# Issuing the attention's loads of later heads from ScalarE's queue instead of SyncE's

## The reference

```
h = RMSNorm(x);  proj = h @ w_in            -> a, gate, q, k, v
group A: u = a*sigmoid(gate); depthwise causal conv (31); LayerNorm; silu; @ w_pw
group B: 8 heads of 64; q, k normed per head; beta = sigmoid(q.k/8)
         A[t,s] = beta[t,s] * prod_{s<j<t} (1 - beta[t,j]),  s < t;   o = A @ v
x = x + concat(A, B) @ w_out;   x = x + relu(RMSNorm(x) @ w_ff1)^2 @ w_ff2
```

## Time and profile before

| | us |
|---|---|
| runs | 2756.15, 2759.61, 2755.06 (median 2756.15) |
| the profiled execution, its own time | 2761.99 |
| its span, first to last instruction | 2760.2 |

### The profile page before, as it was taken

How to read it: one execution, slowest core, us unless ns; L and a number is a source line. 1 busy time by engine, 2 the same in 40 slices (tenths; PEclk the granted TensorE clock), 3 DMA queues, 4 the chain that set the end, 5 groups by cost and what they waited for, 6 DMA issues and landing times. The chain is left out here.

```text
span 2760.2 us, 36720 instructions
## 1 busy us (share of the span) xinstructions
PE 2663.6 (96%) x13304; PEld 2223.3 (81%) x13304; DVE 1797.6 (65%) x2824; ACT 1121.9 (41%) x2221; POOL 592.7 (21%) x523
## 2 busy tenths in 40 slices
PE   8988899999999999999999999999999999999999
PEld 6757778788887887788888797778777877889998
DVE  6996777577773576377775358736888851755444
ACT  4434524455552122355554112334666630333342
POOL 2222210022220010032221002103333310533230
PEclk9999999999999999999999999999999999999999
DMA  9795797697669568455554746854455447355452
GB/s 330 254 351 191 233 354 279 252 332 267 254 219 371 225 228 280 177 218 186 178 181 157 305 183 224 269 197 155 145 191 175 162 161 293 123 189 177 168 198 96
DMA packets 294750, 616.14 MB, mean 223 GB/s; under 512 B 23665, under 2 KB 188529, under 8 KB 250029
## 3 DMA queue, kind: packets, MB, share of 16 engines
q1 hardware_dynamic: 294573, 613.80, 62.8%
HBM read 444.79 MB, written 168.94 MB: 222 GB/s over the span
## 5 line engine op out<-in xcount | busy, mean ns | idle before, releaser
L1277 POOL TENSOR_TENSOR beta<-beta,stay 128x512 f32<-128x512 f32 (+3 forms) x328 | 319.1, 974 | 882.2 <-DVE stay L2047 850.9
L2297 PE MATMUL ps<-h2T_hi,w_s 128*128 128x512 f32 (+2 forms) x976 | 369.6, 379 | 7.6 <-DMA w_s<-w_scratch 3.5
L2299 PE MATMUL ps<-h2T_hi,w_s 128*128 128x512 f32 (+2 forms) x976 | 359.2, 368 | 0.0
L2298 PE MATMUL ps<-h2T_lo,w_s 128*128 128x512 f32 (+2 forms) x976 | 358.7, 367 | 0.0
L1581 ACT ACTIVATE stay<-ps 128x512 f32<-128x512 f32 (+3 forms) x328 | 174.7, 533 | 343.7 <-PE ps L2498 213.3
L2570 PE MATMUL ps<-w_s,hid_hi 128*128 128x512 f32 x768 | 307.2, 400 | 0.0
L2572 PE MATMUL ps<-w_s,hid_hi 128*128 128x512 f32 x768 | 300.1, 391 | 0.0
L2571 PE MATMUL ps<-w_s,hid_lo 128*128 128x512 f32 x768 | 299.6, 390 | 0.0
L2204 DVE TENSOR_TENSOR resid<-ps,resid 128x512 f32<-128x512 f32 x256 | 173.8, 685 | 182.4 <-PE ps L2572 181.9
L2047 DVE TENSOR_TENSOR_SCAN stay<-stay,stay,ones 128x512 f32<-128x512 f32 x192 | 268.7, 1400 | 0.0
L1839 DVE SCALAR_TENSOR_TENSOR cacc<-uT,vecs,cacc 128x512 f32<-128x512 f32 (+1 forms) x360 | 259.7, 777 | 1.5
(11 more groups left out here) (268 smaller groups left out, 5640.6 us busy)
## 6 DMA issues: line engine op xcount, KB each, us to landing
w_s<-w_scratch SPq DMA_DIRECT2D x254, 1024.0 KB, 8.0
w_scratch<-w_s SPq DMA_DIRECT2D x94, 1024.0 KB, 8.6
w_raw<-in_w_ff SPq DMA_DIRECT2D x92, 512.0 KB, 5.4
a_k<-k_scratch SPq DMA_DIRECT2D x80, 256.0 KB, 3.7
a_v<-v_scratch SPq DMA_DIRECT2D x80, 256.0 KB, 4.0
a_q<-q_scratch SPq DMA_DIRECT2D x64, 256.0 KB, 4.2
w_s<-w_scratch SPq DMA_DIRECT2D x28, 512.0 KB, 6.5
w_raw<-in_w_in SPq DMA_DIRECT2D x20, 512.0 KB, 8.1
```

What stands on the lines that cost most here:

```text
L1277: nc.gpsimd.tensor_tensor(v[0:q.r, 0:n], v[0:q.r, 0:n], stay_of(q.z)[0:q.r, 1:n + 1], ALU.mult).then_inc(s_a, 1)
L2297: nc.tensor.matmul(out, w[0], x[0], start=start, stop=False)
L2298: nc.tensor.matmul(out, w[0], x[1], start=False, stop=False)
L2299: return nc.tensor.matmul(out, w[1], x[0], start=False, stop=stop)
```

## The change

Of `att`'s loads on SyncE, all three kinds go to ScalarE. The loads of `att_begin` stay with SyncE, as do all slabs and stores. Of 80 key, 80 value and 64 query loads in all, 69, 69 and 52 move.

- Keys and queries are issued in `att_sigmoids`, right behind the two sigmoids of the piece whose scores were waited for: no wait of their own.
- Values are issued at the head of `att_later`, still six steps after the piece, behind a wait for `v_ps`.
- In chunk 0 keys and values now count on a semaphore for each of the two places (`kv_sem`), where both heads shared the first bank's; `k_loads` counts accordingly. TensorE's waits name the same loads as before.

```diff
+        def kv_sem(c, s, head):
+            return head % 2 if c == 0 else s
         def k_loads(c, s, head):
-            return 16 * (NH * (c - s) + head + 1)
+            return 16 * (head // 2 + 1) if c == 0 else 16 * (NH // 2 * (s < 2) + NH * (c - max(s, 1)) + head + 1)
...
             def att(c, step):                                    # SyncE
-                q = att_piece(c, step, 1)
-                if q and not q.kind:
-                    following = q.head + (1 if c else 2)
-                    if q.p == 1 and q.ends and following < NH:
-                        sp.wait_ge(z_ps, q.z + 1)
-                        load_keys(c, following, q.a0 // BANK)
-                    if q.final:
-                        later = [x for x in ATT[c, 0] if x.hp == q.hp + 3]
-                        if later:
-                            sp.wait_ge(z_ps, q.z + 1)
-                            load_queries(c, later[0])
-                q = att_piece(c, step, VALUES + 1)
-                following = q.head + (1 if c else 2) if q else NH
-                if q and not q.kind and q.p == 1 and q.ends and following < NH:
-                    sp.wait_ge(v_ps, q.v + 1)
-                    load_values(c, following, q.a0 // BANK)
...
             def att_sigmoids(c, step):                           # ScalarE
                 nc.scalar.activation(beta[q.z % 4][0:q.r, 0:q.n], z, ACT.Sigmoid).then_inc(s_sg, 1)
+                if not q.kind:
+                    following = q.head + (1 if c else 2)
+                    if q.p == 1 and q.ends and following < NH:
+                        load_keys(c, following, q.a0 // BANK)
+                    if q.final:
+                        later = [x for x in ATT[c, 0] if x.hp == q.hp + 3]
+                        if later:
+                            load_queries(c, later[0])
             def att_later(c, step):
+                q = att_piece(c, step, VALUES + 1)
+                following = q.head + (1 if c else 2) if q else NH
+                if q and not q.kind and q.p == 1 and q.ends and following < NH:
+                    act.wait_ge(v_ps, q.v + 1)
+                    load_values(c, following, q.a0 // BANK)
```

More of the change, by code:

```diff
@@ L989, in load_keys @@
                 sp.dma_start(a_k[:, at:at + BANK].bitcast(F32),
-                             k_d[head, :, s * BANK:(s + 1) * BANK]).then_inc(k_in[s], 16)
+                             k_d[head, :, s * BANK:(s + 1) * BANK]).then_inc(k_in[kv_sem(c, s, head)], 16)
             def load_values(c, head, s):
                 at = 4 * s + kv_place(c, head) // P
-                sp.dma_start(a_v[:, at:at + 4, :].bitcast(F32), v_d[head, :, 4 * s:4 * s + 4, :]).then_inc(v_in[s], 16)
+                sp.dma_start(a_v[:, at:at + 4, :].bitcast(F32), v_d[head, :, 4 * s:4 * s + 4, :]).then_inc(v_in[kv_sem(c, s, head)], 16)
             def load_queries(c, q):
@@ L1565, in pw, with load_keys, load_values, load_queries @@
                     nc.scalar.copy(pwo[:, ev % 2, 0, 0:w], ps[:, T_BANK + ev % 2, 0:w]).then_inc(pw_hi, 1)
+            def load_keys(c, head, s):
+                at = s * BANK + kv_place(c, head)
+                act.dma_start(a_k[:, at:at + BANK].bitcast(F32),
+                              k_d[head, :, s * BANK:(s + 1) * BANK]).then_inc(k_in[kv_sem(c, s, head)], 16)
+            def load_values(c, head, s):
+                at = 4 * s + kv_place(c, head) // P
+                act.dma_start(a_v[:, at:at + 4, :].bitcast(F32), v_d[head, :, 4 * s:4 * s + 4, :]).then_inc(v_in[kv_sem(c, s, head)], 16)
+            def load_queries(c, q):
+                t = c * CHUNK + 2 * P * q.p
+                act.dma_start(a_q[:, q.hp % 3, :, :].bitcast(F32), q_d[q.head, :, :, t:t + 2 * P]).then_inc(q_in[q.hp % 3], 16)
             def att_sigmoids(c, step):
@@ L2485, in scores @@
                     if q.p == 0 and q.t == 0:
-                        pe.wait_ge(k_in[q.a0 // BANK], k_loads(c, q.a0 // BANK, q.head))
+                        pe.wait_ge(k_in[kv_sem(c, q.a0 // BANK, q.head)], k_loads(c, q.a0 // BANK, q.head))
                     if q.t == 0 and q.diag:
@@ L2518, in values @@
                 elif q.p == 0:
-                    pe.wait_ge(v_in[q.a0 // BANK], k_loads(c, q.a0 // BANK, q.head))
+                    pe.wait_ge(v_in[kv_sem(c, q.a0 // BANK, q.head)], k_loads(c, q.a0 // BANK, q.head))
                 pe.wait_ge(t_lo, q.z + 1)
```

## The result

| | median us | lowest to highest | runs |
|---|---|---|---|
| before | 2756.29 | 2753.32 to 2762.84 | 20 |
| after | 2762.11 | 2759.25 to 2766.54 | 20 |

The ratio is 1.0019 with a 95% interval of 1.0013 to 1.0025: about 5 us slower, where 8.4 us faster was forecast (2748, range 2741 to 2766). The time lies inside the range; the sign is wrong.

A forecast was written before the change was run, and what follows sets the result against it. TensorE, busy 96% of the span, was taken as the bound, with only 96.6 us idle to win. Terms −6.9 − 2.5 − 1.0 + 2.0 = −8.4 us, from the median 2756.15 to 2748, range 2741 to 2766.

The forecast's parts named there:

- the three key waits: TensorE's waits for key transfers, 8.4 us together, 6.0 us the longest; keys queue behind other work on SyncE.
- the first rival: The loads land no sooner: one service order for both queues, waits stay; +1 us, 2757, chance 0.12.
- chunk 1's key waits: TensorE's stops of 0.67 and 1.79 us in chunk 1 go: 2.46 us won, bounds 0 and 2.46.
- the 2.0 us that ScalarE was to pay: Exposed cost of issuing on ScalarE, one us each in first and last chunk; bounds 0 and 19 us.
- No cost: ScalarE's new wait for the values' products names a product done before scores it awaits anyway: no cost.
- The first wait: Chunk 0: TensorE's 5.97 us stall for head 2's keys goes; 6.9 us won, bounds 0 and 8.7.
- half of 317 GB/s: Rate assumed for keys and next query block beside slabs, both queues served in turn: 3.3 us for 0.52 MB.
- What SyncE wins: SyncE loses its waits, runs up to seven steps ahead, slabs may leave a little sooner: 0 us.
- The store behind the slabs: ScalarE's 7.34 us stall for an `ohl` store near 309 us: 1.0 us won, bounds 0 and 7.3.
- ScalarE is held by its issues: Slower rival: up to 19 us of issuing exposed in first and last chunk; 2765 or 2774, chance 0.18.
- Given back inside the first chunk: Rival: later `kqT_second` waits and store stall grow by the keys' gain; −1.5 us, 2754.7, chance 0.12.

The follow-up runs named there:

- e_kv: Changed kernel with the query loads put back on SyncE, keys and values staying on ScalarE; ratio to the kernel before 0.9991.
- e_kq: Changed kernel with the value loads put back on SyncE, keys and queries staying on ScalarE; ratio to the kernel before 0.9980.
- e_wait: Changed kernel with SyncE's old waits for scores and values put back, loads staying on ScalarE; ratio to the kernel before 1.0020.
- b_q2k: Kernel before, all loads on SyncE, with the queries' scratch laid out by blocks of 256 frames (2 KB runs); ratio to the kernel before 0.9992.
- e_vearly: Changed kernel with the values' issue moved up on ScalarE to just behind the sigmoids, ahead of keys and queries; ratio to the kernel before 0.9982.

## Why the prediction was wrong

**What held.** The place and the cause of the three key waits, and that a load on a second queue passes the slabs, which e_kv shows; that excludes the first rival. That the keys landed at 239.5 where 239.4 was forecast is luck: they took 7.5 us instead of 6.2 and were issued 1.3 us sooner than assumed, as the whole stage lay 1.3 us earlier. The slabs that they were to pass had been begun 5 us sooner, counted from the first score product (2.1 us ahead of it, in before 2.9 behind), and had all landed by 238.7, ahead of the keys. The 2.5 us of chunk 1's key waits, to within 0.1 us in e_kq. That ScalarE can issue: an issue takes 0.33 us for keys and values and 0.53 for queries at the median, as on SyncE, and TensorE's waits for `aT` in the last chunk are 6.7 and 7.9 us in two profiles against the 7.8 of the earlier trace rows. Of the 2.0 us that ScalarE was to pay, the part of the last chunk is not there; in the first, the waits for `aT` grew from 1.7 to 3.6 us.

**What failed, in the order of size.**

The values. "No cost" for their wait, and no term for their move: in fact about 10 us, by the ratios of after (1.0019) and e_kq (0.9980). Chunk 1 took 257.9 and 253.2 us in the two profiles after and 247.5 with values on SyncE. I checked what the wait would hold up behind it on ScalarE, and not when ScalarE gets to it, nor what would stand ahead of the load in the new queue. No wait for values appeared in before, and I took that as freedom to move them. It was slack that SyncE's prompt issue had made.

The first wait, −6.9 us: measured −1.0 to −2.2 for the whole of chunk 0's attention. The failing assumption is "half of 317 GB/s". By the counts the engines share their turns by packets, so ScalarE's queue gets half of the packets and an eighth (1 KB) or a fifth (2 KB) of the bytes. The keys came in time nonetheless. The query block before them did not: it had been in front of the slabs, and I costed only the loads that were late, not the one that the move would make late. "What SyncE wins" was wrong with it: "a little sooner" was 5 us for these slabs, so that all four were begun when the block was issued; with SyncE's waits back (e_wait) the wait for this block is 1.2 us, but the next block's is 3.4. With 2 KB packets chunk 0 gains 4.8 to 6.7 us, most of the 6.9, though about 1 us of it may come with the layout alone (b_q2k, 93.5).

The store behind the slabs, −1.0 us: its wait fell by 0.8 to 1.7 us (5.64 and 6.11 in two profiles, 6.87 to 7.34 in before). The size is about right; the reason given for it was not tested.

**The rivals.** "ScalarE is held by its issues" has the sign but not the reason, and e_vearly excludes it. "Given back inside the first chunk" is the nearest for the front by its number, not by its mechanism: the waits for `kqT_second` did not grow (8.5 and 8.2 us after, 8.6 to 10.0 in before), nor did the store's stall. None names what decided: a load that was on time and comes late by the move. The Trainium skill's rule ("DMA: Bandwidth & Descriptors", section "Queues, rings and completion order") that engines go round-robin, a packet at a time, agrees with the counts, 196 against 197. But the packet that the Trainium skill means there holds some 9 to 17 descriptors, and the profile's packets here are single runs of 1, 2 or 8 KB; which of the two takes the turn no run here tells. I quoted the rule and then divided bytes.

## What to carry to other kernels

When loads move to a second queue beside bulk traffic, count the packets and not the bytes: here equally many of either queue moved, and the queue of 1 KB packets beside 8 KB ones got an eighth of the bytes. Make the small loads' runs longer, or keep the slack. Check each load that moves, not only the late one: what stood ahead of it before, what will stand ahead of it now, and when the new engine reaches the issue. A load without a wait may have just enough slack: here 14.9 us, of which 3.2 were used before and 18.6 wanted after.

## What was not expected of the hardware

- Beside running slabs a load on ScalarE's queue moved nothing for some 4 us. The query block of 228.76 us had no packet until 232.6 (in e_kv the keys of 231.57 none until 235.0), while on SyncE a block with nothing ahead of it landed in 3.0 us altogether (that of 230.04 in before). Why, no run here shows. From 228.76 to 232.5 us this row of SyncE's queue is the only one (packets, MB, share):

```profile
q1 hardware_dynamic: 219, 1.54, 98.8%
```

- Stalls of 2.65, 3.74 and 2.73 us on TensorE were followed by 6.83, 3.41 and 3.41 us at the lower clock (0.50, 1.2 GHz): the shortest stall by the longest stretch.
- A single issue on ScalarE took up to 1.85 us, with a query block just ahead of it (594.62 us), and ScalarE stood idle for 0.69 us, until 596.56; on SyncE they went up to 4.84 us.
